# One transformer layer in split fp32: the second half of the MLP, its sums and order on DVE and Pool, and its last chunk by seven products

## The reference

```
x = x + concat(rms(global attention), rms(neighbourhood attention)) @ w_out
u = rms_norm(x, norm_mlp_g) @ w_up            # 1024 -> 4096
u = square(relu(u))
x = x + u @ w_down                            # 4096 -> 1024
y = rms_norm(x, final_norm_g)
```

## Time and profile before

| | us |
|---|---|
| runs | 1192.45, 1195.66, 1192.32 |
| median | 1192.45 |
| the profiled execution, its own time | 1192.22 |
| its span, first to last instruction | 1190.3 |
| PE busy | 1160.2 (97%) |
| DVE busy | 643.9 (54%) |
| ACT busy | 493.5 (41%) |
| Pool busy | 304.2 (26%) |
| PE matmuls | 5696 |
| granted PE clock, mean | 0.998 |

### The profile page before, as it was taken

The page is one execution under the profiler, slowest core; times in us unless marked ns, Lnnn a source line. Parts: engine busy times, 40 slices in busy tenths (PEclk is TensorE's granted clock), DMA queues, the critical chain, the costliest instruction groups (busy, mean ns, idle before and its releaser), DMA issues.

```text
span 1190.3 us, 15287 instructions
## 1 busy us (share of the span) xinstructions
PE 1160.2 (97%) x5696; PEld 956.7 (80%) x5696; DVE 643.9 (54%) x1115; ACT 493.5 (41%) x949; POOL 304.2 (26%) x280
## 2 busy tenths in 40 slices
PE   6999999999999999999999999999999999999997
PEld 5898888799999888886887887887887887878885
DVE  5535223676765645538528439348348257266266
ACT  6421223566675634545243253352442342341134
POOL 2520693122140000104213115015014123131015
PEclk9999999999999999999999999999999999999999
DMA  9421114664434634321201201202202103101105
GB/s 256 112 77 53 45 45 107 145 136 99 93 67 112 160 93 132 112 71 36 89 18 53 71 18 54 80 10 71 63 9 89 54 1 106 36 1 60 47 18 142
DMA packets 51913, 90.45 MB, mean 76 GB/s; under 512 B 5760, under 2 KB 21120, under 8 KB 51840
## 3 DMA queue, kind: packets, MB, share of 16 engines
q1 hardware_dynamic: 51840, 89.47, 27.2%
...
## 4 chain that ended last, share of the span: by engine, by line
PE 86%; DVE 9%; ACT 2%; issue 2%; DMA 0%; ACTq 0%; DVEq 0%
PE ps L922 24%; PE ps L923 24%; PE ps L924 24%; PE ps L1127 5%; DVE uv_lo L1655 3%; DVE w_lo L1634 2%; PE ps L1149 2%; DVE xr L1680 2%; PE ps L821 1%; PE ps L1088 1%; PE ps L1103 1%; PE ps L1089 1%; PE ps L1072 1%; PE ps L1115 1%; ACT uv_hi L1388 1%
## 5 line engine op out<-in xcount | busy, mean ns | idle before, releaser
L922 PE MATMUL ps<-hT,w_hi 128*128 128x512 f32 x640 | 253.4, 396 | 0.0
L924 PE MATMUL ps<-hT,w_lo 128*128 128x512 f32 x640 | 253.1, 396 | 0.0
L923 PE MATMUL ps<-hT,w_hi 128*128 128x512 f32 x640 | 253.1, 395 | 0.0
L869 DVE SCALAR_TENSOR_TENSOR w_lo<-w_raw,w_gain,w_hi 128x512 fp32r<-128x512 f32 (+1 forms) x112 | 88.3, 795 | 177.6 <-ACT w_hi L860 176.7
L860 ACT ACTIVATE w_hi<-w_raw,w_gain 128x512 fp32r<-128x512 f32 (+1 forms) x112 | 78.4, 708 | 221.0 <-PE ps L924 214.8
L922 PE MATMUL ps<-w_hi,uv_hi 128*128 128x512 f32 x392 | 155.1, 396 | 9.8 <-DVE w_lo L1634 9.8
L924 PE MATMUL ps<-w_hi,uv_lo 128*128 128x512 f32 x392 | 155.3, 396 | 0.0
L923 PE MATMUL ps<-w_lo,uv_hi 128*128 128x512 f32 x392 | 154.9, 395 | 0.0
L924 PEld LDWEIGHTS ps<-hT,w_lo 128*128 128x128 f32 x640 | 120.2, 188 | 29.0
L923 PEld LDWEIGHTS ps<-hT,w_hi 128*128 128x128 f32 x640 | 120.3, 188 | 28.9
L922 PEld LDWEIGHTS ps<-hT,w_hi 128*128 128x128 f32 x640 | 120.3, 188 | 28.8
...
## 6 DMA issues: line engine op xcount, KB each, us to landing
w_raw<-w_up SPq DMA_DIRECT2D x72, 256.0 KB, 2.8
b<-w_down SPq DMA_DIRECT2D x56, 256.0 KB, 3.1
w_raw<-w_in SPq DMA_DIRECT2D x48, 256.0 KB, 2.7
stk<-stg SPq DMA_DIRECT2D x32, 256.0 KB, 3.7
w_raw<-w_out SPq DMA_DIRECT2D x32, 256.0 KB, 2.6
...
pj<-x_prompt SPq DMA_DIRECT2D x4, 512.0 KB, 6.6
pj<-x_sample SPq DMA_DIRECT2D x4, 512.0 KB, 13.7
```

What stands on the lines that cost most here:

```text
L869: ins = nc.vector.scalar_tensor_tensor(w_lo[:, slot, 0:width], src, g, hi, ALU.mult, ALU.subtract)
L922: nc.tensor.matmul(out, a_hi, b_hi, start=first, stop=False, skip_group_check=onto)
L923: nc.tensor.matmul(out, a_hi, b_lo, start=False, stop=False, skip_group_check=onto)
L924: return nc.tensor.matmul(out, a_lo, b_hi, start=False, stop=last, skip_group_check=onto)
```

## The change

The change has four parts, all in the MLP.

1. From chunk 1 on, DVE and no longer Pool makes T1, T3, T2 and S3, and in all chunks the low parts of S4 and A22: 12 operations a chunk. Pool keeps S4 and T4. In chunk 0 Pool still makes T1, T3, T2 and S3.
2. DVE's order in a chunk: the additions `add_x(c, 0)` and `add_x(c, 1)` stand behind `down_low` of v2 and v3 instead of ahead of them; `add_x(c, 2)` stands ahead of v4's `down_low` as before, followed by the low part of S4. In chunk 0 v1's second weight tile is split ahead of the last hidden squares. Pool's S4 waits for v2's weights to be split on DVE.
3. The last chunk also has a down phase of seven products, in the order v0, v1, v2, v3, v5, v4, v6 (`LAST_ORDER`). With v5 the rows of sequence 0 are complete: DVE and ACT finish them (square, root, reciprocal, scaling) while PE does v4 and v6. The finish is in half rows of 512 columns: the half that is complete first is multiplied by the gain on Pool (`gain_early`) and scaled there (sequence 0) or on ACT (sequence 1), the later one is done by one operation on DVE (`finish`). Sixteen stores of 256 KB replace eight of 512 KB.
4. The final gain is loaded once, at the start of chunk 1, into `out_gain`.

```diff
+LAST_ORDER = (0, 1, 2, 3, 5, 4, 6)
+def place(c, v):
+    return LAST_ORDER.index(v) if c == NCHUNK - 1 else v
-S_CH = NCHUNK - 1
+S_CH = NCHUNK
...
@@ PE, down_products
-                product(c, 4, 0, added(2), False, True)
-                product(c, 5, 4, added(3), False, True)
+                if c == NCHUNK - 1:
+                    product(c, 5, 4, added(3), False, True)
+                    product(c, 4, 0, added(2), False, True)
+                else:
+                    product(c, 4, 0, added(2), False, True)
+                    product(c, 5, 4, added(3), False, True)
                 product(c, 6, 0, added(4), False, True)
...
@@ ACT
+            def last_down_high():
+                c = NCHUNK - 1
+                down_high(c, 5, 0)
+                down_high(c, 5, 1)
+                u_high(c, "A22")
+                for t in range(TPB):
+                    final_square(t, False)
+                nc.scalar.activation(rms[:, 3, 0, 1:2], eps[:, 0:1], ACT.Sqrt)
+                down_high(c, 4, 0)
+                down_high(c, 4, 1)
+                for t in range(TPB):
+                    if t == TPB - 1:
+                        down_high(c, 6, 0)
+                        down_high(c, 6, 1)
+                    final_square(t, True)
+                    final_root(t)
+                for t in range(TPB, NT):
+                    final_square(t, False)
...
-                    squares(0, 4, 8)
+                    squares(0, 4, 6)
+                    down_high(0, 1, 1)
+                    squares(0, 6, 8)
...
+            for t in range(TPB, NT + 1):
+                if t < NT:
+                    final_square(t, True)
+                    final_root(t)
+                if t > TPB:
+                    act.wait_ge(rstd_ready, norm_no(3, t))
+                    act.wait_ge(xg_ready, t)
+                    cols = half_of(t - 1, False)
+                    nc.scalar.mul(yo[:, t - 1, cols], yo[:, t - 1, cols], rstd[:, 3, t - 1, 0:1]).then_inc(early_out, 1)
...
@@ DVE
+            def half_mean(b):
+                dve.wait_ge(sumsq, SQ0[3] + 2 * TPB * b + TPB)
+                tiles = slice(b * TPB, (b + 1) * TPB)
+                nc.vector.tensor_scalar(half_ms[:, tiles], stat[:, 3, tiles, 0], 1.0 / D, EPS, ALU.mult,
+                                        ALU.add).then_inc(half_ready, 1)
+            def finish(t):
+                dve.wait_ge(rms_ready, norm_no(3, t) + 1)
+                nc.vector.reciprocal(rstd[:, 3, t, 0:1], rms[:, 3, t, 0:1]).then_inc(rstd_ready, 1)
+                dve.wait_ge(rstd_ready, norm_no(3, t) + 1)
+                dve.wait_ge(c_added, added_of(t, True))
+                cols = half_of(t, True)
+                nc.vector.scalar_tensor_tensor(yo[:, t, cols], xr[:, t, cols], rstd[:, 3, t, 0:1], out_gain[:, cols],
+                                               ALU.mult, ALU.mult).then_inc(late_out, 1)
+            def last_down_low():
+                c = NCHUNK - 1
+                down_low(c, 5, 0)
+                down_low(c, 5, 1)
+                u_low(c, "A22")
+                add_x(c, 3)
+                down_low(c, 4, 0)
+                down_low(c, 4, 1)
+                half_mean(0)
+                dve.wait_ge(gain_landed, 32)
+                for t in range(TPB):
+                    add_x(c, 5, (t,))
+                    if t:
+                        finish(t - 1)
+                down_low(c, 6, 0)
+                down_low(c, 6, 1)
+                finish(TPB - 1)
+                add_x(c, 4)
+                half_mean(1)
+                for t in range(TPB):
+                    add_x(c, 6, (t,))
+                    if t:
+                        finish(TPB + t - 1)
+                finish(NT - 1)
...
                 up_low(c, 7)
+                sum_s3(c)
                 u_low(c, "S3")
                 down_low(c, 0, 0)
                 down_low(c, 0, 1)
+                sum_t(c)
+                sum_t2(c)
...
@@ Pool
-            for c in range(S_CH):
-                sum_t(c)
-                if c:
-                    sum_s3(c)
-                sum_t2(c)
-                if c == 0:
-                    sum_s3(c)
-                pool.wait_ge(uv_lo_ready, low_no(c, "S2", 1) + 1)
+            sum_t()
+            sum_t2()
+            sum_s3()
+            for c in range(S_CH):
+                pool.wait_ge(lo_split, down_piece(c, 2, 1) + 1)
                 sum_s4(c)
-                pool.wait_ge(lo_split, down_piece(c, 2, 1) + 1)
-                u_low(c, "S4")
                 pool.wait_ge(lo_split, down_piece(c, 3, 1) + 1)
                 sum_t4(c)
-                pool.wait_ge(lo_split, down_piece(c, 4, 1) + 1)
-                u_low(c, "A22")
...
+            for t in range(TPB):
+                gain_early(t)
+            for t in range(TPB):
+                pool.wait_ge(xg_ready, t + 1)
+                pool.wait_ge(rstd_ready, norm_no(3, t) + 1)
+                cols = half_of(t, False)
+                nc.gpsimd.tensor_scalar(yo[:, t, cols], yo[:, t, cols], rstd[:, 3, t, 0:1], None,
+                                        ALU.mult).then_inc(early_out, 1)
+            for t in range(TPB, NT):
+                gain_early(t)
```

More of the change, by code:

```diff
@@ L175 @@
 PRODUCTS = ["A11", "A12", "S2", "S1", "S3", "S4", "A22"]
-POOL_LOW = ("S4", "A22")
 def hi_order(c):
     return ("A11 A12 S2 S1 S3 S4 A22" if c == 0 else "A11 S3 A12 S2 S1 S4 A22").split()
-def low_no(c, name, kt):
-    names = POOL_LOW if name in POOL_LOW else [x for x in hi_order(c) if x not in POOL_LOW]
-    return 2 * len(names) * c + 2 * list(names).index(name) + kt
 def high_no(c, name, kt):
@@ L226, in add_no @@
 def add_no(c, v, t):
-    return TPB * (VERS * c + v) + t
+    return TPB * (VERS * c + place(c, v)) + t
 def bank_added(c, bank):
@@ L870, in dve_split @@
             ins.then_inc(lo_split, 1)
-        def last_gain(k):
-            return w_gain[:, 2, k:k + 1] if k < DT else None
         def evac_dst(blk, t):
@@ L1669, in sum_s2, with add_x @@
                                         ALU.subtract).then_inc(s12_done, 1)
-            def add_x(c, v):
+            def add_x(c, v, tiles=range(TPB)):
                 b, half = ((0, 0), (0, 0), (0, 1), (1, 1), (1, 1), (0, 1), (1, 0))[v]
-                for t in range(TPB):
+                for t in tiles:
                     dve.wait_ge(down_full, full_down(c, v, t))
```

282 lines of the change are left out of this document (95 added, 187 removed).

## The result

| | before | changed |
|---|---|---|
| median, us | 1193.5 (1192.3 to 1195.7, 7 runs) | 1186.73 (1185.22 to 1189.9, 7 runs) |
| ratio | | 0.9945, 95% interval 0.9927 to 0.9962 |
| profiled execution, own time | 1192.22 | 1185.34 |
| its span | 1190.3 | 1183.5 |
| v0 of chunk 0 starts | 536.7 | 537.7 |

The kernel is faster by 6.9 us in the profiled execution, where 10.4 were forecast. That execution, at 1185.34, lies just inside the range of 1177.0 to 1185.8; the median, at 1186.73, lies above it. The last three rows say where the 6.9 come from: 10.8 us gained up to the last chunk (forecast 10.4), 3.0 lost in it (forecast 0), and 1.0 in the stretch before the MLP, which the change doesn't touch.

What follows compares the result with a forecast made beforehand. The prediction took PE, busy 97% of the span, to bound the kernel. Gains of 8.4 (chunks 1 to 6), 2.0 (chunk 0) and 0 (last chunk), 10.4 us off 1192.2, gave 1181.8 us; range 1177.0 to 1185.8.

Steps and rivals of the forecast that it cites:

- the stall of 1.40: Chunks 1 to 6, PE ahead of v3, waiting for its weights' low part: gone six times, 8.4 us gained.
- C: Rival: v4 inherits the wait, each chunk keeping a stall of 0.7, 4.2 us lost, 1186; chance 0.07.
- D: Rival: DVE's SBUF operations are slow without Pool too, DVE becomes the bound, 13.2 us slower, 1205; chance 0.03.
- E: Rival: the moved order doesn't touch v3's stall, only the last chunk changes, 1190 to 1192; chance 0.02.
- the row of DVE operations that the forecast counted: Chunk 0: DVE's additions, S3 and S4 put v4's weights at 23.7 against 22.4; v4 waits 1.5 us.
- v5 starts near 22.9 instead of 22.4.: Last chunk: v5's weights, third and fourth of six DVE operations with two Pool turns between, set its start.
- Only now may v6 start, at 39.0.: Last chunk: DVE must finish sequence 0 before v6's inputs; PE is free at 34.1, a wait of 4.9 us.
- the three turns that Pool's scalings were to take from DVE: Last chunk, finishes of sequence 0 and v6's weights: three Pool scalings of 1.25 us each delay DVE.
- that case: Last chunk: Pool's scaling takes no turns, three of 1.25 go, v6 starts near 36, giving 1179.
- The sign that was asked for: Last chunk: PE waits 4 to 5 us ahead of v6, not for w_lo but for an addition (xr).
- Rival B, the clock: Last chunk: PE's clock falls during the wait ahead of v6 and slows v6, 1184.5; chance 0.15.
- Rival A: Last chunk: finish of sequence 0 is hidden, Pool's turns falling beside additions, 4.5 us faster, 1177.3; chance 0.2.

Runs made afterwards that it cites:

- the two single edits: Kernel before with DVE's new order alone, 1185.41 us; kernel before with the new shares alone (plus v1's earlier split, Pool's later S4), 1183.69 us.
- e11_s4_later: Chunk 0's S4 low part behind v4's weights, against e3_slot_add with half_mean later, v4's first addition before the last finish, 512 KB stores; 1180.24 us.
- e2_add_first: Changed kernel with v3's four additions ahead of A22's low part in the last chunk; 1185.26 us, ratio to before 0.9929.
- e3_slot_add: Changed kernel with the edits of both e1_slot and e2_add_first; 1181.51 us, ratio to before 0.99.
- e5_slot_add_hold: e3_slot_add with Pool's gain products in the last chunk held back until A22's low part is made; 1182.01 us, ratio to before 0.9907.
- e1_slot: Changed kernel with v6's weights waiting for v5, which really used their slot, instead of v4; 1184.81 us, ratio to before 0.9918.
- e12_best: e11_s4_later with sixteen stores of 256 KB instead of the 512 KB stores for sequence 1; 1180.94 us, ratio to before 0.9892.

## Why the prediction was right and where it was wrong

**Chunks 1 to 6, right.** Forecast: the stall of 1.40 is gone six times, 8.4 us, and the period of a chunk is 84.0. Measured: no stall in any of them, a period of 83.98, and 6 by 1.42 = 8.5 us gained. Chunk 3 of the changed kernel runs as it was laid out: low part of S2 done 7.1 us after v0 (forecast 7.0), v3's weights 13.4 (13.7), wanted at 16.8. The pair of v3's weights, beside no Pool work, takes 1.29 where the earlier trace rows had 2.38. (The prediction put the end of v3's weights in the kernel before at 812.93; the earlier trace rows give 810.63 + 2.38 = 813.01. Nothing hangs on it.) The forecast named both causes (additions ahead, turns with Pool); the two single edits show that it is enough to remove either, which the forecast did not say. Rivals C, D and E are out: no wait ahead of v4 in chunks 1 to 6, DVE's pairs of SBUF operations at 1.28 to 1.47 and not 2.3, and the stall gone.

**Chunk 0, right.** Forecast: one stall ahead of v4, 1.5 us, gain 2.0. Measured: one stall of 1.08 ahead of v4, and from v0 to the next v0 85.3 us instead of 87.6, a gain of 2.3. And e11_s4_later shows it to be the row of DVE operations that the forecast counted.

**The last chunk, wrong, in two steps of the sum and by a third loss that stood only in a rival.** The forecast had two losses on PE, 0.5 ahead of v5 and 4.9 ahead of v6: 5.4. Measured are 2.7, 4.1 and 1.5: 8.3. So 2.2 us more were lost ahead of v5, 0.8 less ahead of v6, and 1.5 by the clock, 2.9 in all. The tail behind the last matmul's start was forecast at 9.3 (53.7 less 44.4) and took 9.3; so the 3.0 us by which the chunk missed its forecast are all PE's. That the tail is right is partly luck, since two errors cancel in it: to the end of the last scaling it took 3.9 us (forecast 4.8), and from there to the end 5.3 (forecast 4.5).

1. *"v5 starts near 22.9 instead of 22.4."* It started at 25.1. That step took v5 to need only its weights. v5 accumulates onto v3's banks, and each tile waits for v3's addition. Everywhere else v4 stands between v3 and v5 and covers that; with `LAST_ORDER` v5 follows v3 directly. v3's additions stood behind v5's weights and A22's low part, at 24.2 to 26.7. The forecast's own layout had them at 24.4 to 26.8: the numbers were there, and the dependency too (v5 accumulates onto v3's), but it was not applied to the new order. e2_add_first and e3_slot_add show it: additions earlier by a pair, v5 earlier by 1.2. The other 1.3 us of the wait are Pool's turns on DVE ahead of v5's weights, as e5_slot_add_hold shows. They made 22.9 early for the weights too: with both turns ahead of them, 18.5, four operations of 0.6 and two turns of 1.15 are 23.2, and they ended at 23.1.

2. *"Only now may v6 start, at 39.0."* The wait was forecast at 4.9 and measured 4.1, near enough to look right, but for another reason. The third finish ended at 1159.80 + 0.75 = 1160.55, 33.6 after v0, and DVE then stood idle for 3.61 us: the three turns that Pool's scalings were to take from DVE never came (L1678 took 0.75 beside them). The prediction had priced that case too, at 1179 with v6 near 36, though its own three turns of 1.25 off 39.0 give 35.3; the slot hid it. v6's weights waited for their slot. The sign that was asked for, a wait of 4 to 5 us for an addition (xr), came true all the same, since v4's first addition stands behind those weights in DVE's row. e1_slot removes the wait by changing nothing but that slot. The wrong line, in `free_slot`, is not in the diff; the diff made it wrong by giving `full_down` a new meaning.

3. **Rival B, the clock, happened,** on top of the forecast and not in its place, and cost 1.5 us: a wait of 4 us was in the sum, and the fall behind it stood only in a rival at 0.15. Its time, 1184.5, came nearest to the profiled 1185.34, but partly by chance: it lacks the 2.2 us that v5's wait took beyond the forecast, and it charged 2.7 for a fall that cost 1.5. The Trainium skill (TensorE: Matmul & The Clock Gate, "Part 1: The HAM clock gate") says that the half rate is the state after idling and that it takes sustained work to leave it; v6's matmuls, 0.43 us apart until 1170.52, agree.

**The rest.** 1.0 us is the start of the MLP, which moves from execution to execution. The sum with what was measured: 1181.8 - 0.4 + 3.0 + 1.0 = 1185.4, against 1185.34. The median, 1186.73, is another 1.4 higher. The forecast was laid on one profiled execution with 0.25 us between it and the median, and the seven runs before have their median 1.3 above it, at 1193.5.

**Rival A** (the finish of sequence 0 is hidden) was half true: DVE was not late in the changed kernel, since Pool's scalings took no turns there. But the slot and v5's wait stood in its place. e12_best, with both mended, ends 51.0 after v0, 2.6 below the direct last chunk, where A had asked for 4.5.

**Part 4 and the up phase.** Costed at nothing, and nothing is seen: DVE's six T operations and two for S3 delayed no v0 in chunks 1 to 6.
